# A second attention mixer issued between the expert slots of one long run of tiles

## What is computed

```
for layer in range(2):
    need_ctx = layer == 0
    a = modulate(rmsnorm(h), shift1, scale1)
    h += gate1 * mixer(a)      # layer 0: retention + short convolution; layer 1: windowed attention
    f = modulate(rmsnorm(h), shift2, scale2)
    h += gate2 * peer_ffn(f)   # layer 1: latent tokens only
out = rmsnorm(h_latent)
```

## Time and profile before

| | |
|---|---|
| median of three runs | 4135.48 us |
| the profiled execution: own time, span of its instructions | 4131.19 us, 4129.2 us |
| PE, DVE, ACT, POOL busy | 69%, 64%, 35%, 38% of the span |
| indirect gathers | 1280 of 1.05 MB, 1342.31 MB |
| other DMA traffic (queue q1) | 110.72 MB |
| first and last `dot` of layer 0 start | 537.71 us, 2467.88 us |
| first and last `dot` of layer 1 start | 2820.68 us, 4106.09 us |

### The profile page before, as it was taken

The page is one execution under the profiler, slowest core; times in us unless marked ns, Lnnn a source line. Parts: engine busy times, 40 slices in busy tenths (PEclk is TensorE's granted clock), DMA queues, the critical chain, the costliest instruction groups (busy, mean ns, idle before and its releaser), DMA issues. The chain is left out here.

```text
span 4129.2 us, 42686 instructions
## 1 busy us (share of the span) xinstructions
PE 2847.3 (69%) x14856; PEld 950.9 (23%) x14856; DVE 2646.5 (64%) x6059; ACT 1438.8 (35%) x4394; POOL 1560.1 (38%) x1482
## 2 busy tenths in 40 slices
PE   4998865666567667567667667886666766766665
PEld 0794611111111111111111116662111111111110
DVE  3314398866866865875874444648886687587444
ACT  2220143343343343333333332533334334333333
POOL 0005044444543444443444421323444444444432
PEclk7999987687778768768666668998766767866665
DMA  8117289999999999999999983027999999999997
GB/s 360 51 62 276 107 364 403 421 421 421 417 420 421 419 413 421 414 413 420 416 416 421 421 353 105 11 82 316 400 421 421 421 420 419 421 419 416 421 421 320
DMA packets 215432, 1455.87 MB, mean 353 GB/s; under 512 B 25920, under 2 KB 25920, under 8 KB 44080
## 3 DMA queue, kind: packets, MB, share of 16 engines
q0 software_dynamic: 184704, 1342.31, 78.5%
q1 hardware_dynamic: 30400, 110.72, 7.3%
q10 hardware_dynamic: 112, 0.11, 0.0%
HBM read 1447.72 MB, written 5.34 MB: 352 GB/s over the span
## 5 line engine op out<-in xcount | busy, mean ns | idle before, releaser
L1474 PE MATMUL peer_py<-peer_ring,peer_diag 64*64 64x512 f32 x10240 | 1957.7, 865 | 1113.6 <-ACT peer_diag L1403 1107.2
L1574 DVE CUSTOM_DVE_ANT_0 peer_ring<-peer_ring,peer_f 128x1024 f32<-128x1024 f32 x1280 | 1555.1, 1225 | 908.6 <-DMA peer_ring<-in_uv_dram,peer_idx 900.4
L1356 POOL DMA_INDIRECT peer_ring<-in_uv_dram,peer_idx x1280 | 1411.5, 1103 | 1856.8 <-PE peer_py L1474 1722.0
L1474 PEld LDWEIGHTS peer_py<-peer_ring,peer_diag 64*64 64x64 f32 x10240 | 359.2, 170 | 2663.3 <-ACT peer_diag L1403 2531.3
L1397 ACT ACTIVATE peer_gel<-peer_u 128x1 f32<-128x1 f32 x1280 | 258.8, 202 | 1900.3 <-DVE peer_u L1574 1900.0
L1403 ACT ACTIVATE peer_diag<-peer_stack,peer_coef 128x64 f32<-128x64 f32 x1280 | 445.1, 348 | 41.7
L1401 ACT ACTIVATE peer_coef<-peer_gel,peer_gate 128x1 f32<-128x1 f32 x1280 | 377.1, 295 | 46.7 <-ACT peer_gel L1397 0.4
L353 DVE TENSOR_TENSOR m_w_low<-m_w_low_plain,m_w_high 128x2048 fp32r<-128x2048 f32 x26 | 61.0, 2348 | 218.5 <-ACT m_w_high L348 218.5
L1449 PE MATMUL peer_pb<-arena,peer_fT 128*128 128x512 f32 x320 | 180.4, 662 | 2.4 <-ACT peer_fT L1370 2.4
L361 PE MATMUL m_ps<-m_w_high,m_aT_high 128*128 128x512 f32 x416 | 165.3, 397 | 4.2 <-DVE m_v L820 1.7
L361 PE MATMUL m_ps<-m_w_low,m_aT_high 128*128 128x512 f32 x416 | 163.4, 393 | 0.0
(11 more groups left out here) (195 smaller groups left out, 2386.4 us busy)
## 6 DMA issues: line engine op xcount, KB each, us to landing
mod_rows_sb<-in_ada_w_dram SPq DMA_DIRECT2D x33, 1024.0 KB, 5.0
peer_ring<-in_uv_dram,peer_idx POOLq DMA_INDIRECT x1280, 15.3
arena<-in_ada_w_dram SPq DMA_DIRECT2D x15, 1024.0 KB, 15.9
m_w_low_plain<-in_ev_w_in_dram SPq DMA_DIRECT2D x12, 1024.0 KB, 5.2
arena<-in_peer_wq_dram SPq DMA_DIRECT2D x2, 4096.0 KB, 19.2
mod_rows_sb<-mod_rows SPq DMA_DIRECT2D x7, 1024.0 KB, 7.0
m_w_low_plain<-in_od_w_in_dram SPq DMA_DIRECT2D x6, 1024.0 KB, 5.4
m_w_low_plain<-in_ev_w_out_dram SPq DMA_DIRECT2D x4, 1024.0 KB, 5.1
```

What stands on the lines that cost most here:

```text
L1356: pool.indirect_dma_start(ring[:, n % RING], None, A["uv"], bass.IndirectOffsetOnAxis(idx[:, i % 2, hd, k:k + 1], 0)).then_inc(sem(f"lande ...
L1474: ins = pe.matmul(PY[strip(c), i % 2, r], diag[strip(r), n % RING], ring[strip(r), n % RING, D + c * HALF:D + (c + 1) * HALF], start=s == ...
L1574: dve.tensor_tensor_reduce(x, x, f[:, i % 2], 1.0, 0.0, ALU.mult, ALU.add, u[:, n % RING:n % RING + 1]).then_inc(sem("dot"), 1)
```

## The change

**One run.** The two expert stages become one, `trunk_stage`: ten tiles, 6 of layer 0 and then 4 of layer 1 (`run_tile`, `run_layer`), with no block between them. Tile 6, the first of layer 1, is routed between the slots of tile 5 like any next tile.

**The mixer alongside.** The second mixer has no stage. Each engine gets a second program (`mixer`), a generator that names the slot behind which its next instructions are issued (`Alongside.upto`). With (tile, slot): the norms start at (2,5), (2,15), (3,5), (4,4), (5,5), (5,100) and (6,4); the nine projections start at (2,27), (3,17), (4,15), (4,21), (4,32), (5,17), (6,15), (6,21) and (6,32) and issue three matmuls in two slots; the attention of the four blocks starts at (4,50), (5,30), (6,50) and (7,8), one pair of heads in 5 slots, 40 slots to a block; the output projection of a block starts 54 slots after its attention, again three matmuls in two slots.

**Plain fp32, weights in pieces.** The projections are single fp32 matmuls of 128 x 128 by 512, with no split. A weight piece is 128 rows by 512 columns, 256 KB, loaded by SP in two DMAs of 64 rows of 2 KB. Four pieces fit (`W_RING`, in space that the modulation rows of the context had). 9 projections of 8 pieces and 4 output projections of 16 pieces make 136 pieces, 35.65 MB; the kernel before read 10.49 MB for the same, since key and value weights are now read for each group of tiles and the output weights for each block. `wq` of layer 1 (4.19 MB), its keys (0.52 MB), modulation rows, the mixer's gate row and the rope tables (3.93 MB together) are now also loaded during the run.

**Space.** `RING` is 7. `PY` has one buffer: PE waits in slot 0 of a tile until DVE has taken the sum of the tile before (`gather_sum`, in slot 1; `add_up` adds it to `h` in slot 2). PSUM gives 2 banks to the sums, 2 to the routing (4 before) and 4 to the mixer. The routing forms both halves of the queries before it transposes them, and the scores in two halves, the second behind slot 45; the 32 search pieces go from slot 47 on (53 in the first tile), with a gap of two places in the middle.

**ACT.** `weight` is two instructions, Gelu of the diagonal (scale = the dot product) and a multiplication by the gate.

The core of the diff:

```diff
-RING = 8
+RING = 7
+PR = 4
-ACT_SQUARE, DVE_MEAN, ACT_ROOT, DVE_MOD = 1, 3, 5, 8
-PE_F_T, ACT_F_T, PE_Q = 11, 14, 16
+ACT_SQUARE, DVE_MEAN, ACT_ROOT, DVE_MOD = 3, 5, 7, 10
+PE_F_T, ACT_F_T, PE_Q = 13, 15, 17
+PRODUCTS = ((KV, ((0, 0, 0), (1, 1, 1)), at(2, 27)), (KV, ((2, 0, 0),), at(3, 17)), (KV, ((3, 1, 0),), at(4, 15)),
+            (Q0, ((2, 0, 1), (3, 1, 3)), at(4, 21)), (Q1, ((2, 0, 0), (3, 1, 2)), at(4, 32)), (KV, ((4, 0, 0),), at(5, 17)),
+            (KV, ((5, 1, 0),), at(6, 15)), (Q0, ((4, 0, 1), (5, 1, 3)), at(6, 21)), (Q1, ((4, 0, 0), (5, 1, 2)), at(6, 32)))
+ATTENDS = (at(4, 50), at(5, 30), at(6, 50), at(7, 8))
+STEP = 5
+W_RING = 4
+class Alongside:
+    def upto(self, slot):
+        while self.slot <= slot:
+            self.slot = next(self.program, NEVER)
...
+            def in_pieces(c):
+                for k in range(KC):
+                    to, loaded = next_slot()
+                    for x in range(2):
+                        at_row = k * P + x * HD
+                        sp.dma_start(to[x * HD:(x + 1) * HD], A["od_w_in"][0][at_row:at_row + HD, c * HALF:(c + 1) * HALF]
+                                     ).then_inc(loaded, 16)
...
             def weight(i, s):
                 act.wait_ge(sem("dot"), n + 1)
-                act.activation(gel[:, at], u[:, at], ACT.Gelu).then_inc(sem("gelu"), 1)
+                act.activation(diag[:, n % RING], stack[:], ACT.Gelu, scale=u[:, n % RING:n % RING + 1]).then_inc(sem("gelu"), 1)
                 if k == 0:
                     act.wait_ge(sem("gate"), batch_ready(i, hd))
-                act.activation(coef[:, at], gel[:, at], ACT.Copy, scale=gate[:, i % 2, hd, k:k + 1]).then_inc(sem("coef"), 1)
-                act.activation(diag[:, n % RING], stack[:], ACT.Copy, scale=coef[:, at]).then_inc(sem("diag"), 1)
+                act.activation(diag[:, n % RING], diag[:, n % RING], ACT.Copy, scale=gate[:, i % 2, hd, k:k + 1]).then_inc(sem("diag"), 1)
...
             def combine(i, s):
-                if s == 0 and i >= 2:
-                    pe.wait_ge(sem("y"), i - 1)
+                if s == 0 and i >= 1:
+                    pe.wait_ge(sem("y"), i)
...
+            def exps(b, m):
+                for i in (2 * p, 2 * p + 1):
+                    act.wait_ge(S("mix_logits"), i + 1)
+                    act.activation(pr[:, i % PR, 0:n], pr[:, i % PR, 0:n], ACT.Exp, bias=st[:, 0, i:i + 1], scale=-1.0,
+                                   accum_out=st[:, 1, i:i + 1]).then_inc(S("mix_probs"), 1)
...
-        peer_stage(nc, S, A, h, ident, mod_d, arena, rows, 0, 0, 0, NT)
-        mixer1_stage(nc, S, A, h, ident, mod_d, arena, rows)
-        peer_stage(nc, S, A, h, ident, mod_d, arena, rows, 1, CT, NT, LT)
+        trunk_stage(nc, S, A, h, ident, mod_d, arena, rows)
```

More of the change, by code:

```diff
@@ L1262, in next_piece, with batch_ending, batch_ready @@
+def next_piece(i, s):
+    for m in range(NH * PIECES):
+        if i < RUN - 1 and piece_slot(i, m) == s:
             return divmod(m, PIECES)
     return None
-def peer_stage(nc, S, A, h, ident, mod_d, arena, rows, layer, t0, first, n_tiles):
+def batch_ending(i, piece):
+    if piece is None or piece[1] != PIECES - 1:
+        return None
+    ends = [hi - 1 for lo, hi in gates_of(i)]
+    return ends.index(piece[0]) if piece[0] in ends else None
+def batch_ready(i, hd):
+    before = sum(len(gates_of(j)) for j in range(i))
+    return before + [n for n, (lo, hi) in enumerate(gates_of(i)) if lo <= hd < hi][0] + 1
@@ new lines, with __init__, merged, at @@
+NEVER = RUN * TS
+class Alongside:
+    def __init__(self, program):
+        self.program = program
+        self.slot = next(program)
+    def upto(self, slot):
+        while self.slot <= slot:
+            self.slot = next(self.program, NEVER)
+def merged(*programs):
+    slots = [next(x, NEVER) for x in programs]
+    while min(slots) < NEVER:
+        x = slots.index(min(slots))
+        yield slots[x]
+        slots[x] = next(programs[x], NEVER)
+def at(i, s):
+    return i * TS + s
+BAND = P + 2 * 128
@@ L1347, in _ @@
             pool.iota(iota[:], [[1, TOPK]], base=0, channel_multiplier=0, allow_small_or_imprecise_dtypes=True
                       ).then_inc(sem("iota"), 1)
-            for i in range(first, last + 1):
+            other = Alongside(mixer())
+            for i in range(RUN):
                 for s in range(TS):
@@ L1415, in _ @@
+            square(0)
+            root(0)
+            f_turned(0)
+            query(0, 0)
+            query(0, 1)
+            queries_turned(0)
+            scored(0, 0)
+            exponents(0, 0)
+            act.wait_ge(S("mix_cols_ps"), 1)
+            act.activation(cols[:].rearrange("p c s k -> p (c s k)"), PM[:, 0, 0:2 * 3 * KC], ACT.Copy).then_inc(S("mix_cols"), 1)
+            act.wait_ge(sem("stack"), 1)
+            other = Alongside(mixer())
+            for i in range(RUN):
                 for s in range(TS):
@@ L1596, in _ @@
-            dve.wait_ge(sem("idx"), first * NH + LAG)
-            below_top(first, 0)
-            normalise(first, 0)
-            for i in range(first, last + 1):
+                    route(0, hd, piece)
+            dve.wait_ge(sem("idx"), LAG)
+            below_top(0, 0)
+            normalise(0, 0)
+            other = Alongside(mixer())
+            for i in range(RUN):
                 for s in range(TS):
                     dot(i, s)
-                    if i > first and s == 4:
+                    if i > 0 and s == 1:
+                        gather_sum(i - 1)
+                    if i > 0 and s == 2:
```

1063 lines of the change are left out of this document (600 added, 463 removed).

## The result

The median fell from 4135.6 to 4097.0 us (four runs, 4092.5 to 4102.6), a ratio of 0.9913 with an interval of 0.990 to 0.9926. The kernel is faster by 0.9%, where 4.1% was predicted, and 4097 lies above the range of 3905 to 4080. The profiled execution has a span of 4090.8 us.

What follows compares the result with a forecast made beforehand. DMA bytes were taken to set the plateaus, with a hole between the layers. 4131.2 - 346 + 9 + 114 + 21 + 12 + 20 = 3961, with 4.3 for the median 3965 us; range 3905 to 4080.

Steps and rivals of the forecast that it cites:

- hole: Second mixer and routing between the layers, DMA engines used to 0.18; closing it was put at -346 us net.
- start: First tile: both query halves are formed before anything is transposed, put at +9 us.
- bytes of `wq`, rows and tables: Loads once read in the hole, now read while DMA engines are full: 8.6 MB at 421 GB/s, +21 us.
- The round-trip rival: Gather ring: buffer round trip is latency, so 7 buffers give 2.88 us a slot; 4259 us, chance 0.07.
- Bytes: Weight pieces and other loads on full DMA engines: pieces 93 us at 382 GB/s, the rest 21, together +114.
- The rival of half rows: Piece DMAs to 64 partitions run at half rate, so pieces cost 187 us, not 93; 4058 us, chance 0.07.
- No cost in throughput: ACT in the mixer's attention: a pair of heads needs 10.6 us of the 12.5 in 5 slots, so 0 us.
- my terms for PE and DVE: PE, slots with query products and projections: +21 (0 to 50). DVE, attention over routing: +12 (0 to 40).
- Waits: Table excursions, POOL divisions, tile ends and pieces delay gathers, five queued gathers cover 12 us; +20, between 0 and 116.
- The output projections (1.5 pieces a slot, 3.5 us) are set by DMA, not by PE: PE term: output projections take 3.5 us a slot, set by DMA.
- The rival of starved pieces: Projections run at the landing of pieces, not their bytes: 116 us in place of 20; 4061 us, chance 0.15.

Runs made afterwards that it cites:

- no_mixer: Changed kernel with the second mixer's programs empty on all engines and its pieces not loaded; ring of 7 kept: 3808.9 us.
- compute_alone: Changed kernel with only the first four pieces loaded, PE's empty last attention step removed, and Relu and Square for the mixer's exponentials: 3863.9 us.
- no_exp_tables: whole_no_tail with Relu and Square in place of the mixer's two exponentials, so no change of ACT's function table: 3942.8 us.
- whole_no_tail: Changed kernel with one DMA of 128 partitions per piece and PE's empty last attention step removed: 3982.3 us.
- whole_pieces: Changed kernel with one DMA of 128 partitions per piece in place of two of 64, output weight rows reordered: 4011.8 us.
- no_loads: Changed kernel with only the first four weight pieces loaded, later products reusing those buffers; all mixer instructions kept: 3908.5 us.
- column_halves: Changed kernel with each piece still two DMAs, but each to 128 partitions by 256 columns; output rows ordered as in whole_pieces: 4026.5 us.
- pairs_of_pieces: whole_paced with two neighbouring pieces brought by one DMA, 4 KB to a partition, buffers freed two by two: 3971.3 us.
- whole_paced: whole_no_tail with one product per slot, not three in two, for projections with one tile to a piece: 3967.1 us.

## Why the prediction was wrong

One path leads from `no_mixer` to the changed kernel with one step at a time. Each row is the difference of two medians; the steps depend on their order, as shown above, and each is uncertain by about 10 us.

| step | measured | predicted |
|---|---|---|
| before to no_mixer: hole, start, bytes of `wq`, rows and tables | -326.7 (to 3808.9) | -346 + 9 + 21 = -316 |
| no_mixer to compute_alone: all the mixer's instructions, but no table changes, no tail | +55.0 (3863.9) | +21 + 12 = +33 |
| compute_alone to no_exp_tables: whole pieces loaded | +78.9 (3942.8) | +93 |
| to whole_no_tail: change of tables | +39.5 (3982.3) | 0 |
| to whole_pieces: the tail | +29.5 (4011.8) | +20, all waits |
| to the changed kernel: half rows | +85.2 (4097.0) | 0 |

**The hole, the start, the ring.** Right. Against -316 stand -326.7. The first dot product starts at 547.1, 9.4 us later than before, where 9 was forecast. The round-trip rival is out: with seven buffers tile 8 takes 322.0 us. The mixer keeps its slots, and the hole does not open again.

**Bytes: the main step that failed.** The prediction said: "At 382 the pieces cost 93 us." For whole pieces that holds (79). But 382 came from the earlier trace rows, where every load covers 128 partitions, and was applied to loads that cover 64. The rival of half rows put their price at 187 and got 0.07: 94 more for them, where 85.2 were measured. `no_loads` gives 188.5 for the loads with all their waits, and `whole_pieces` and `column_halves` name the cause. That the rival's 4058 and the tables' 39.5 make just the measured 4097 is luck: the table's other misses, -10.7, +22, -14.1, +9.5 and -8.8, happen to cancel. The reason given against the rival, that both halves of a piece and gathers to all partitions are under way at once, does not help: the gathers are slowed too. In tile 4 they run at 380 GB/s of their own share, where whole pieces leave them 398. The rule of the Trainium skill (SBUF — State Buffer, Door 1: The DMA port swizzle), that a transfer to partitions 0 to 63 reaches 8 of 16 ports, gave the right order of size here, beside other traffic as well; the runs agree with it, though they don't show ports. When rows are silent on a form of transfer, silence is no evidence against a rule that is stated for it.

**ACT: "No cost in throughput".** The sum of 10.6 us in 12.5 was not too low: in the 40 slots of the first block's attention, 2039.6 to 2161.0, ACT is busy for 67.3 us, 8.4 for each five. Nor was 1.28 for a table load. This is the second step that failed, a term put at nothing that measured 39.5: a sum over five slots was held against the pace. ACT stands in the chain dot, diagonal, combine, free slot, gather, and an uninterrupted 4.5 us in it is more than a slot. The prediction saw this under *Waits* and let five queued gathers cover it; they did not, since each pair takes another bite before the queue has filled again while pieces and routing fill the DMA engines and DVE. That last is argued; the 39.5 are measured. The Trainium skill (ScalarE: Activation LUTs, What ACT_TABLE_LOAD costs) puts a drain of 1.38 us beside each load. No row here has it: the first exponential starts at 2062.26, 0.01 us behind the end of the load.

**PE.** Where query products and projections with two tiles to a piece meet, PE runs without idle time. Four slots with four query products and six of the projection take 13.45 us, so 3.36 a slot for the predicted 3.65; a product takes 0.94 there in the mean, not 1.05:

```profile
1963.31 1.09 PE L1422 MATMUL peer_py<-peer_ring,peer_diag 64*64 64x512 f32 x8
1964.33 1.12 PE L1392 MATMUL peer_pb<-arena,peer_fT 128*128 128x512 f32 x2
1965.29 1.02 PE L1462 MATMUL mix_ps<-mod_rows_sb,peer_mix_aT 128*128 128x512 f32 x2
1966.24 1.09 PE L1422 MATMUL peer_py<-peer_ring,peer_diag 64*64 64x512 f32 x8
...
1970.04 1.09 PE L1422 MATMUL peer_py<-peer_ring,peer_diag 64*64 64x512 f32 x8
...
1976.76 1.09 PE L1422 MATMUL peer_py<-peer_ring,peer_diag 64*64 64x512 f32 x8
```

The mechanism was right, and the slot somewhat shorter than predicted. The 55 us are 22 more than my terms for PE and DVE, within their upper ends (50 and 40), but what ACT and POOL do for the mixer is in them too. In `compute_alone` the tiles 4 to 7 account for 43: they take 347.3, 328.3, 347.8 and 326.2 us against 336.2, 324.0, 323.6 and 322.4 in `no_mixer`. How the 55 divide between the engines was not measured.

**Waits, and the output projections.** "The output projections (1.5 pieces a slot, 3.5 us) are set by DMA, not by PE" took the pace of the slots from `out_slot` and missed the order of the generator, which issues eight at once. The rival of starved pieces was half right: its place was there, and PE waited 67.5 + 35.1 us for pieces. With whole pieces 41.0 + 22.7 are left, so over a third of it came from half rows and the larger part did not. There the tail is worth 29.5 us and the pace 15.2 more, 44.7 together, where the prediction had 20 for all waits.

## What to carry to other kernels

Read the DMA share together with GB/s: a share of 0.96 at 353 GB/s is a loss that the share alone hides. Then look for its cause with a kernel that leaves the suspect out: without the pieces it was still 0.95 at 371. Write a tile with DMAs to all 128 partitions, also when another full stream runs beside it. An engine at a third of its time can set the pace if it works in pieces longer than a slot, so hold the longest uninterrupted stretch against the slack, not the sum; and when programs of generators are merged, look for the steps that issue nothing but still hold a slot.

## What the runs showed of the hardware

Half-partition writes slow the traffic beside them. The 136 pieces as halves of 64 partitions cost 188.5 us with the waits for them, against 35.65 MB / 421 GB/s = 85 for their bytes, and 85 of it went away with one DMA to all partitions. The gathers beside them ran at 380 GB/s of their own share with half rows, 398 with whole pieces, 396 with the mixer but all pieces after the fourth left out, and 413 to 415 with no mixer work. Beside gathers a whole piece of 262 KB landed every 3.1 us and a piece in two halves every 4 to 5, though alone at 421 GB/s it would take 0.6. That packets of queues take turns would explain it; the one run meant for that (`pairs_of_pieces`) does not bear it out, since PE waited longer for its pieces than in `whole_paced`.

A change of ACT's function table took 1.283 us each time, with no more than 0.02 us before and behind it, and 32 excursions of 4.5 us cost 39.5 us on an engine that was busy for a third of the span.
